# The last LayerNorm of the sample rows laid out over 128 partitions instead of 8

## The chip, the core and the metric

The kernel runs on one core of one Trainium2 chip. Its engines are TensorE (PE, matrix products), VectorE (DVE), ScalarE (ACT), GpSimd (POOL) and SyncE (SP, which here only issues DMAs). DMAs are issued by SP, ACT and POOL. The metric is the device time of one launch in microseconds (us), as the median of the runs.

## The reference, cut to what matters

One step of a one-layer decoder trunk: a mixer, a cross-attention into 256 memory tokens and a mixture of experts, with a LayerNorm behind each. It runs for a prompt of 512 tokens and for 8 sample tokens (520 rows of D = 1024 columns). The change touches only the end: the sum of each token's two experts, the residual and the last LayerNorm.

```
def layer_norm(x, g, b):
    mu = x.mean(-1, keepdims=True)
    var = jnp.mean(jnp.square(x - mu), -1, keepdims=True)
    return (x - mu) * lax.rsqrt(var + 1e-5) * g + b

x = layer_norm(ALPHA * x + hier_moe(x, p), p['ln3_g'], p['ln3_b'])
```

Each token has two chosen experts, and `hier_moe` is the weighted sum of their two outputs.

## The kernel before, in words

Tokens lie in rows. The 512 prompt rows are four tiles of 128 partitions (`t` = 0, 1, 2, 4), and the 8 sample rows are a tile of their own, number 3 (`SAMPLES`), which uses 8 of the 128 partitions. `xn[:, t, :]` holds the rows of tile `t`.

The experts run in 11 passes of 128 slots each. The outputs of the first nine passes are scattered to a table `y_d` in DRAM, one row per token and choice. The outputs of the last two passes (`KEPT`) stay in SBUF (`ysb`), and TensorE adds them to their tokens with selection matrices `places` (`add_kept` for a prompt tile, `add_samples` for the samples). A `sum_full` count tells when a bank of such sums is ready.

The rows of `y_d` reach `xn` in two ways. POOL issues accumulating DMAs (`accumulate(c, t)`, `c` is the first or second choice) in the order samples, 0, 1, 2 for the first choice, then the samples' second, tile 4's first, tile 2's second and tile 4's second; some of them wait for the landing of an earlier one of the same tile. The second choice of tiles 0 and 1 is loaded by SP into `second_choice` and added by VectorE. The semaphore `x3_in[t]` counts the landings of tile `t`.

Then comes the last norm, in the order `LAST_NORM = [0, 3, 1, 2, 4]`. For each tile VectorE adds the kept sums to `xn` in two halves of 512 columns and sums the rows in the same instruction (`tensor_tensor_reduce`, L2676). It forms minus the mean (L2681) and (x − mean)·gain (L2683). ScalarE squares with the mean as bias and sums (L1794), takes the root (L1796) and, once VectorE has the reciprocal (L2658), scales the centred rows (L1800). In the program of VectorE the reciprocal of a tile stands behind the first half of the next tile. POOL stores each scaled tile with an accumulating DMA onto output rows that already hold the bias (L3023). The last tile, 4, takes another way: VectorE scales and adds the bias in two halves (L2694), and SP and ACT store a half each (L1368, L1803).

The kept sums of the samples stand in one PSUM bank as four column groups: columns 256g to 256g + 255 of the 8 samples are on partitions 32g to 32g + 7 (L1190). Before the samples' norm, ScalarE copies two of the groups (L1790) and VectorE the other two (L2687) to 8 partitions of 1024 columns (`late_samples`).

Of the kernel before, what the change touches and what calls it, by code (L numbers as in the profile page):

```python
# [22 lines left out]
D = 1024  # L23
# [8 lines left out]
LAST_NORM = [0, 3, 1, 2, 4]  # L32
# [53 lines left out]
def rows_of(t):  # L86
    return NS if t == SAMPLES else TR
# [34 lines left out]
def layer_kernel(nc, a, o):  # L122
# [3 lines left out]
    with ctx:  # L126
# [142 lines left out]
        late_samples = P[0:NS, NT * D:(NT + 1) * D]  # L269
        zeros = view(16094, 256)  # L270
        places = smp[:, 1120:1120 + KEPT * NTOK].rearrange("p (i c) -> p i c", i=KEPT)
        tokens16 = smp[:, 2162:2162 + KEPT]
# [5 lines left out]
        kept_sums = lambda t, q: (1 if t == 0 else 2) + kept_bank(t, q)  # L278
        SAMPLES_SUM = 3
# [209 lines left out]
        def _(pe):  # L489
# [698 lines left out]
            def add_samples(i, bank):  # L1188
                for g in range(4):
                    last = mm(bank[32 * g:32 * g + NS, 0:256], places[:, i, NP_:NTOK], ysb[:, (NSCAT + i) % 3, g * 256:g * 256 + 256],  # L1190
                              start=(i == 0), stop=(i == KEPT - 1))
                return last

            pe.wait_ge(places_ready, KEPT)
# [6 lines left out]
            for t in PROMPT:  # L1201
                if t == 4:
                    pe.wait_ge(y_act, NPASS + 1)
                    pe.wait_ge(y_dve, NPASS + 1)
# [5 lines left out]
                if t == 0:  # L1210
                    add_samples(1, ps[6]).then_inc(sum_full, 1)

# [26 lines left out]
        def _(sp):  # L1239
# [129 lines left out]
            with sp.If(over > 0):  # L1369
                sp.wait_ge(x_out, 16)  # L1370
                sp.wait_ge(half_out, 16)
                sp.wait_ge(rows_out, 16 * NQT)
# [32 lines left out]
            sp.wait_ge(rows_out, 16 * NQT)  # L1405
# [11 lines left out]
        def _(act):  # L1417
# [367 lines left out]
            for i, t in enumerate(LAST_NORM):  # L1785
                n = rows_of(t)
                if t == 0:
                    act.wait_ge(sum_full, SAMPLES_SUM)
                    for g in range(2):
                        last = A(late_samples[:, g * 256:g * 256 + 256], ps[6][32 * g:32 * g + NS, 0:256], ACT.Copy)  # L1790
                    last.then_inc(y_act, 1)
                act.wait_ge(x3_mean, i + 1)
                r = rstd[0:n, t:t + 1]
                A(squares[0:n, :], xn[0:n, t, :], ACT.Square, bias=mean3[0:n, t:t + 1], accum_out=square3[0:n, t:t + 1]).then_inc(x3_square, 1)  # L1794
                act.wait_ge(x3_square, i + 2)
                A(r, square3[0:n, t:t + 1], ACT.Sqrt, scale=1.0 / D, bias=eps[0:n, :]).then_inc(x3_root, 1)  # L1796
                if i < NT - 1:
                    act.wait_ge(x3_rstd, i + 1)
                    act.wait_ge(x3_centred, i + 1)
                    A(centred3[0:n, t, :], centred3[0:n, t, :], ACT.Copy, scale=r).then_inc(x3_scaled, 1)  # L1800
# [23 lines left out]
        def _(dve):  # L1824
# [799 lines left out]
            def place_rows(i):  # L2624
                p = NSCAT + i
                dve.wait_ge(*entry_landed(p))
# [3 lines left out]
                for t in range(NT):  # L2630
                    n = rows_of(t)
# [19 lines left out]
            dve.wait_ge(gb_in, 96)  # L2651
            dve.wait_ge(xa_ready, NT)

            def take_root(i):
                t = LAST_NORM[i]
                r = rstd[0:rows_of(t), t:t + 1]
                dve.wait_ge(x3_root, i + 1)
                V.reciprocal(r, r).then_inc(x3_rstd, 1)  # L2658

            for i, t in enumerate(LAST_NORM):  # L2660
                n = rows_of(t)
                x, r = xn[0:n, t, :], rstd[0:n, t:t + 1]
                centred = centred3[0:n, t, :]
# [3 lines left out]
                for q in range(2):  # L2667
                    lo, hi = q * 512, q * 512 + 512
                    if t == SAMPLES:
                        dve.wait_ge(y_act, NPASS + 1)  # L2670
                        dve.wait_ge(y_dve, NPASS + 1)
                        total_q = late_samples[:, lo:hi]
                    else:
                        dve.wait_ge(sum_full, kept_sums(t, q))
                        total_q = ps[kept_bank(t, q)][:, :]
                    V.tensor_tensor_reduce(out=x[:, lo:hi], in0=x[:, lo:hi], in1=total_q, scale=1.0, scalar=0.0,  # L2676
                                           op0=ALU.add, op1=ALU.add, accum_out=part3[0:n, t, q:q + 1]).then_inc(row_parts, 1)
                    if q == 0 and i > 0:
                        take_root(i - 1)
                dve.wait_ge(row_parts, 2 * i + 2)  # L2680
                V.tensor_scalar(mean3[0:n, t:t + 1], part3[0:n, t, 0:1], part3[0:n, t, 1:2], -1.0 / D, ALU.add, ALU.mult).then_inc(x3_mean, 1)  # L2681
                dve.wait_ge(x3_mean, i + 1)
                V.scalar_tensor_tensor(centred, x, mean3[0:n, t:t + 1], gb[0:n, 0, :], ALU.add, ALU.mult).then_inc(x3_centred, 1)  # L2683
                if i == 0:
                    dve.wait_ge(sum_full, SAMPLES_SUM)
                    for g in (2, 3):
                        last = V.tensor_copy(late_samples[:, g * 256:g * 256 + 256], ps[6][32 * g:32 * g + NS, 0:256])  # L2687
                    last.then_inc(y_dve, 1)
                if i == NT - 1:
                    take_root(i)  # L2690
# [378 lines left out]
```

## Time and profile before

| | us |
|---|---|
| median of 3 runs | 646.45 (646.26 to 646.46) |
| the profiled execution | 650.46 |
| span of its trace | 648.6 |
| VectorE starts the first row sum of the last norm | 625.12 |
| VectorE starts with tiles 1, 2 and 4 | 631.98, 634.82, 637.66 |
| ScalarE starts the last square | 639.51 |
| ACT issues the last store | 642.81 |

All times of instructions are microseconds from the start of the span. TensorE is busy for 95% of the span, but it is done with its last sum at 635.87; the last norm, at the end, belongs to VectorE, ScalarE and the DMAs.

### The profile page before, as it was taken

The numbers are of one execution on the slowest core, as the hardware profiler recorded it, in microseconds if no ns is written. First come the engines' busy times: TensorE is split into PE (matmuls) and PEld (weight loads), VectorE is DVE, ScalarE is ACT, GpSimd is POOL, SyncE is SP. The second block draws the span as 40 slices with busy tenths as digits, with TensorE's granted clock in tenths as the row PEclk, the third lists the DMA queues.
The fourth block names the chain that finished last, engine by engine and source line by source line (L and its number), as shares of the span: only waits on it lengthen the run. The fifth ranks groups of instructions, "written<-read, shape, count | busy, mean of one in ns | idle before, by whom it ended". The sixth has DMA issues, their size and how long they took to land.

```text
span 648.6 us, 8964 instructions
## 1 busy us (share of the span) xinstructions
PE 615.8 (95%) x3319; PEld 394.6 (61%) x3319; DVE 366.7 (57%) x845; ACT 164.4 (25%) x367; POOL 204.6 (32%) x248
## 2 busy tenths in 40 slices
PE   6899999999999979999999999999999999999992
PEld 3588788887888854446888784454574443333230
DVE  1485898326556863557653874257885342443465
ACT  1175211002544120002001740221433111212144
POOL 7050010100677735312000986011324731110221
PEclk9999999999999989999999999999999999999997
DMA  8995678616335354003904985354998999999898
GB/s 278 364 312 171 235 169 229 240 51 211 118 94 214 130 195 148 16 0 107 348 1 128 340 310 200 134 225 161 369 415 326 406 411 366 334 411 418 323 185 162
DMA packets 49175, 150.08 MB, mean 231 GB/s; under 512 B 5498, under 2 KB 8250, under 8 KB 44897
## 3 DMA queue, kind: packets, MB, share of 16 engines
q1 hardware_dynamic: 35159, 112.48, 46.6%
q0 software_dynamic: 11232, 31.76, 17.4%
q10 hardware_dynamic: 2738, 5.23, 2.1%
q8 instruction: 28, 0.46, 0.3%
q14 instruction: 18, 0.15, 0.1%
HBM read 131.83 MB, written 21.90 MB: 237 GB/s over the span
## 4 chain that ended last, share of the span: by engine, by line
PE 74%; DMA 12%; DVE 7%; POOL 2%; issue 2%; SPq 2%; ACT 1%; DVEq 0%; POOLq 0%; ACTq 0%
PE ps L611 14%; PE ps L788 14%; PE ps L609 9%; PE ps L1148 7%; PE ps L517 5%; PE ps L1168 4%; DMA xn<-in_x_sample 2%; PE ps L807 2%; PE ps L890 2%; PE ps L584 2%; PE ps L874 2%; DMA xn<-y_d 1%; DMA P<-x_d,smp 1%; SPq L1273 1%; DMA wring<-in_ca_wq 1%
## 5 line engine op out<-in xcount | busy, mean ns | idle before, releaser
L788 PE MATMUL ps<-wring,P 128*128 128x512 f32 x224 | 99.2, 596 | 0.0
L788 PEld LDWEIGHTS ps<-wring,P 128*128 128x128 f32 x224 | 41.6, 190 | 49.1 <-issue 49.0
L1926 DVE SCALAR_TENSOR_TENSOR P<-ps,P 128x256 f32<-128x256 f32 (+1 forms) x83 | 33.8, 424 | 57.2 <-PE ps L611 36.6
L1148 PE MATMUL ps<-wring,P 128*32 128x512 f32 (+1 forms) x320 | 63.6, 593 | 0.9 <-DVE P L2600 0.9
L517 PE MATMUL ps<-xT,wring 128*128 128x312 f32 (+1 forms) x256 | 57.4, 383 | 0.0
L517 PEld LDWEIGHTS ps<-xT,wring 128*128 128x128 f32 x256 | 46.4, 190 | 9.3
L2600 DVE COPY P<-ps 128x512 f32<-128x512 f32 x10 | 6.9, 692 | 63.5 <-PE ps L1129 63.5
L1148 PEld LDWEIGHTS ps<-wring,P 128*32 128x32 f32 (+1 forms) x320 | 20.4, 122 | 31.0 <-issue 30.9
L2922 POOL TENSOR_TENSOR P<-P,xT 128x2048 f32<-128x2048 f32 x8 | 36.0, 4521 | 9.2 <-DMA xT<-sq_d 5.4
L2774 POOL TENSOR_SCALAR rstd<-agg 128x1 f32<-128x1 f32 (+1 forms) x10 | 12.0, 1195 | 85.3 <-DVE agg L1856 85.3
L2234 DVE SCALAR_TENSOR_TENSOR xn<-xn,ps 128x512 f32<-128x512 f32 x16 | 11.0, 684 | 42.1 <-PE ps L788 31.1
L1168 PE MATMUL ps<-P 128*32 128x512 f32 (+1 forms) x160 | 32.6, 595 | 0.7 <-issue 0.7
L609 PE MATMUL ps<-wring,P 128*128 128x256 f32 x128 | 31.1, 395 | 2.2 <-DVE wring L1901 2.2
L611 PE MATMUL ps<-xT,wring 128*128 128x264 f32 (+1 forms) x128 | 29.7, 387 | 0.1
L611 PE MATMUL ps<-P 128*128 128x264 f32 x128 | 29.5, 385 | 0.0
L611 PE MATMUL ps<-P,wring 128*128 128x256 f32 (+1 forms) x128 | 29.2, 382 | 0.0
L609 PEld LDWEIGHTS ps<-wring,P 128*128 128x128 f32 x128 | 24.7, 197 | 6.4 <-DVE wring L1901 2.6
L611 PEld LDWEIGHTS ps<-xT,wring 128*128 128x128 f32 x128 | 23.8, 190 | 5.0 <-issue 1.1
L611 PEld LDWEIGHTS ps<-P 128*128 128x128 f32 x128 | 24.3, 190 | 4.2
L1479 ACT ACTIVATE xT<-ps 128x512 f32<-128x512 f32 (+1 forms) x20 | 9.5, 515 | 67.4 <-PE ps L584 67.2
L611 PEld LDWEIGHTS ps<-P,wring 128*128 128x128 f32 x128 | 24.2, 190 | 3.8
L609 PE MATMUL ps<-P 128*128 128x256 f32 x104 | 24.3, 381 | 0.0
(480 smaller groups left out, 1157.1 us busy)
## 6 DMA issues: line engine op xcount, KB each, us to landing
wring<-in_w_in SPq DMA_DIRECT2D x5, 2048.0 KB, 9.7
wring<-in_w_gate SPq DMA_DIRECT2D x10, 1024.0 KB, 8.3
wring<-in_w_up SPq DMA_DIRECT2D x10, 1024.0 KB, 11.2
P<-in_w_down SPq DMA_DIRECT2D x10, 1024.0 KB, 11.6
P<-in_cache_mem_k SPq DMA_DIRECT2D x8, 1024.0 KB, 7.0
P<-in_cache_mem_v SPq DMA_DIRECT2D x8, 1024.0 KB, 4.9
y_d<-P POOLq DMA_DIRECT2D x1, 4160.0 KB, 32.1
wring<-in_ca_wv SPq DMA_DIRECT2D x2, 2048.0 KB, 20.0
```

The costliest lines, as they stand in the source:

```text
L517: last = mm(out, lhs(k), rhs(k), start=(k == 0), stop=(k == n - 1))
L584: last = nc.tensor.transpose(bk[:, k * n:k * n + n], xn[0:n, t, (4 * q + k) * 128:(4 * q + k + 1) * 128], ident[0:n, 0:n])
L609: last = mm(bank[:, 0:n], x[:, k, 128 * i:128 * i + 128], w[:, k, :], start=(k == 0), stop=(k == 3))
L611: last = mm(bank[:, 0:n], w[:, k, 128 * i:128 * i + 128], x[:, k, :], start=(k == 0), stop=(k == 3))
L788: last = mm(bk[:, :], src[:, k, START[t]:START[t] + TR], w[:, k, :], start=(k == 0), stop=(k == KC - 1))
L807: last = mm(bank[:, :], mixT[:, k, 0:TR], w[:, k, :], start=(k == 4), stop=(k == 1))
L874: last = mm(bk[:, 0:NM], qcT[:, 2 * h + k, t * TR:t * TR + TR], mkT[:, 2 * h + k, :], start=(k == 0), stop=(k == 1))
L890: last = mm(bk[:, 0:cn], mv[:, m, h * CE + ec * 128:h * CE + ec * 128 + 128], paT[:, h, m, c0:c0 + cn], start=(m == 0), stop=(m == 1))
L1148: last = mm(GU[p % 2][lo:lo + m, :].rearrange("p (g f) -> p g f", g=2), xgT[:, p % 3, k, lo:lo + m], gu[s][:, :, k, :], start=(k == 0), st ...
L1168: last = mm(YB[q][lo:lo + m, :], hT[:, p % 2, f, lo:lo + m], dn[s][:, f, q * 512:q * 512 + 512], start=(f == 0), stop=(f == 1))
L1926: V.scalar_tensor_tensor(dst, src, scale, part, ALU.mult, ALU.add).then_inc(part_added, 1)
L2922: G.tensor_tensor(x, x, qb[:, b % 4:b % 4 + 1].broadcast_to([128, 2, D]), ALU.mult).then_inc(kq_done, 1)
```

## The change

The samples' last norm is done in the layout in which TensorE leaves their sums: 128 partitions of 256 columns, where partitions 32g to 32g + 7 hold column group g and the other 24 partitions of each group hold zeros. The samples are third in the order: `LAST_NORM = [0, 1, 3, 2, 4]`.

- SP copies the samples' rows from `xn` to `samples_s` (128 x 256) by four SBUF-to-SBUF DMAs of 8 x 256, once the second choice has landed in them. VectorE waits for all four (`RELAID`) ahead of tile 1.
- The four copies by ScalarE and VectorE to `late_samples` are gone. VectorE adds `samples_s` and the PSUM bank in one 128 x 256 instruction ahead of tile 1.
- A row's sum is now spread over four partitions. `sum_lanes` adds the four parts on TensorE: the product of the matrix `same_lane` (1 where two partitions are equal modulo 32) with one column. This is done once for the mean, behind tile 1's sums, and once for the squares, ahead of tile 4's sums. TensorE waits for VectorE (`row_parts`) and for ScalarE (`x3_square`) before them.
- ScalarE's order is written out: the samples' square stands ahead of tile 1's scale, their root behind it, and their scale ahead of tile 2's.
- POOL sets `samples_s` to zero and loads the gain in the new layout (`gain_s`, four DMAs) during the expert passes. VectorE forms `same_lane` in the pass where it makes `places`.
- The samples are stored by four accumulating DMAs of 8 x 256 behind those of tiles 0, 1 and 2.

```
-LAST_NORM = [0, 3, 1, 2, 4]
+LAST_NORM = [0, 1, 3, 2, 4]
...
-        kept_sums = lambda t, q: (1 if t == 0 else 2) + kept_bank(t, q)
+        kept_sums = lambda t, q: {0: 1, 1: 4, 2: 7, 4: 10}[t] + q
+        SAMPLES_SUM, SAMPLES_MEAN, SAMPLES_VAR = 3, 6, 9
...
+            def sum_lanes(column, parts):
+                mm(ps[0][:, column:column + 1], same_lane, parts, start=True, stop=True).then_inc(sum_full, 1)
...
                 if t == 4:
-                    pe.wait_ge(y_act, NPASS + 1)
-                    pe.wait_ge(y_dve, NPASS + 1)
+                    pe.wait_ge(x3_square, 4)
+                    sum_lanes(1, square3[:, SAMPLES:SAMPLES + 1])
...
+                if t == 1:
+                    pe.wait_ge(row_parts, SAMPLES_ADDED)
+                    sum_lanes(0, part3[:, SAMPLES, 0:1])
...
+            sp.wait_ge(choice_in[1], 16)
+            sp.wait_ge(x3_in[SAMPLES], loads_of(SAMPLES))
+            for g in range(4):
+                sp.dma_start(samples_s[lanes(g), :], xn[0:NS, SAMPLES, quarter_of(g)]).then_inc(choice_in[1], 16)
...
+                if t == SAMPLES:
+                    dve.wait_ge(sum_full, SAMPLES_MEAN)
+                    V.tensor_scalar(mean, ps[0][:, 0:1], -1.0 / D, None, ALU.mult).then_inc(x3_mean, 1)
+                    dve.wait_ge(x3_mean, i + 1)
+                    V.scalar_tensor_tensor(centred_s, samples_s, mean, gain_s, ALU.add, ALU.mult).then_inc(x3_centred, 1)
+                    continue
+                if t == 1:
+                    dve.wait_ge(choice_in[1], RELAID)
+                    dve.wait_ge(sum_full, SAMPLES_SUM)
+                    add_rows(samples_s, ps[6][:, 0:256], part3[:, SAMPLES, 0:1])
...
+            link(G.memset(samples_s, 0.0))
+            for g in range(4):
+                pool.dma_start(gain_s[LANES * g:LANES * g + LANES, :], a["ln3_g"][0, quarter_of(g)].partition_broadcast(LANES)).then_inc(gb_in, 16)
...
+            for i, t in ((0, 0), (1, 1), (3, 2)):
                 pool.wait_ge(x3_scaled, i + 1)
+                pool.dma_start(o_xp[0, START[t]:START[t] + TR, :], centred3[:, t, :], accum_op=ALU.add).then_inc(rows_out, 16)
+            for g in range(4):
+                pool.dma_start(o_xs.rearrange("b one d -> (b one) d")[:, quarter_of(g)], centred_s[lanes(g), :], accum_op=ALU.add).then_inc(rows_out, 16)
```

On VectorE, behind the centring of tile 0 and up to the first half of tile 1, the program before has these rows (`ISA` with `ps` or `P` as its second operand is the add with row sum; the `ISA` behind it reads the sum out):

```order
L2687 COPY P<-ps 8x256 [waits sum_full]
L2687 COPY P<-ps 8x256
L2676 ISA xn,smp<-xn,P 8x512 [waits y_dve,y_act,x3_in3]
L2676 ISA smp 8x1
L2658 RECIPROCAL rstd<-rstd 128x1 [waits x3_root]
L2676 ISA xn,smp<-xn,P 8x512 [waits y_dve,y_act]
L2676 ISA smp 8x1
L2681 TENSOR_SCALAR smp<-smp 8x1 [waits row_parts]
L2683 SCALAR_TENSOR_TENSOR P<-xn,smp,gb 8x1024 [waits x3_mean]
L2676 ISA xn,smp<-xn,ps 128x512 [waits sum_full,choice_added,x3_in1]
```

On VectorE at the same place, from behind the centring of tile 0 to the first half of tile 2, the program after has these:

```order
L2701 ISA smp<-smp,ps 128x256 [waits sum_full,choice_in1]
L2701 ISA smp 128x1
L2701 ISA xn,smp<-xn,ps 128x512 [waits sum_full,choice_added,x3_in1]
L2701 ISA smp 128x1
L2698 RECIPROCAL rstd<-rstd 128x1 [waits x3_root]
L2701 ISA xn,smp<-xn,ps 128x512 [waits sum_full]
L2701 ISA smp 128x1
L2727 TENSOR_SCALAR smp<-smp 128x1 [waits row_parts]
L2729 SCALAR_TENSOR_TENSOR P<-xn,smp,gb 128x1024 [waits x3_mean]
L2708 TENSOR_SCALAR smp<-ps 128x1 [waits sum_full]
L2710 SCALAR_TENSOR_TENSOR P<-smp 128x256 [waits x3_mean]
L2701 ISA xn,smp<-xn,ps 128x512 [waits sum_full,x3_in2]
```

Nine instructions between tile 0 and tile 1 have become two, with a wait for `choice_in1`, and two small ones stand between tile 1 and tile 2. The reciprocal of tile 0 has moved behind the first half of tile 1. (In the program after, L2701 is the line of `add_rows`, and L2708 and L2710 are the samples' mean and centring.)

On SP, between the loads of the second choice (L1374) and the store of the last tile (L1384), the program after has these:

```order
L1374 DMA wring<-y_d 128x1024 [waits y_out1,y_out2,y_out0,gu_full]
L1374 DMA wring<-y_d 128x1024
L1378 DMA smp<-xn 8x256 [waits x3_in3,choice_in1]
L1378 DMA smp<-xn 8x256 x3
L1381 TENSOR_LOAD flag [waits sorted_ready]
L1381 ISA x2
L1384 DMA out<-P 128x512 [waits last_ready]
```

The two rows of L1378 are new; before, the load of the flag followed the second choice at once.

## Rows read from the trace of the kernel before

**Rows 1.** Chain that ended last: start us, us, what.
```profile
637.66 0.68 DVE xn L2676
...
640.77 0.30 ACT rstd L1796
```

**Rows 2.** Timeline, tile 1: start us, us, engine, line, operation, out<-in, count.
```profile
631.98 0.69 DVE L2676 CUSTOM_DVE_ANT_0 xn<-xn,ps 128x512 f32<-128x512 f32 x1
...
632.59 0.15 DVE L2658 RECIPROCAL rstd<-rstd 8x1 f32<-8x1 f32 x1
...
633.37 0.21 DVE L2681 TENSOR_SCALAR smp<-smp 128x1 f32<-128x1 f32 x1
...
633.83 1.13 ACT L1794 ACTIVATE P<-xn,smp 128x1024 f32<-128x1024 f32 x1
...
634.82 0.68 DVE L2676 CUSTOM_DVE_ANT_0 xn<-xn,ps 128x512 f32<-128x512 f32 x1
```

**Rows 3.** Timeline, the samples on VectorE.
```profile
628.02 0.85 DVE L2687 COPY P<-ps 8x256 f32<-8x256 f32 x2
```

**Rows 4.** Timeline, the last tile.
```profile
639.51 1.14 ACT L1794 ACTIVATE P<-xn,smp 128x1024 f32<-128x1024 f32 x1
...
642.81 0.34 ACTq L1803 DMA_DIRECT2D out<-P  x1
```

**Rows 5.** Timeline and DMA issues: out<-in queue op count, KB, us to landing.
```profile
618.66 1.69 POOL L3007 DMA_DIRECT2D xn<-y_d  x2 [2.01 <-DMA xn<-y_d]
...
xn<-y_d POOLq DMA_DIRECT2D x1, 32.0 KB, 8.8
```

**Rows 6.** Timeline and DMA issues, copies of other sizes.
```profile
612.47 0.82 SPq L1362 DMA_DIRECT2D wring<-y_d  x2
...
qk_d<-smp POOLq DMA_DIRECT2D x2, 16.0 KB, 1.8
...
wring<-y_d SPq DMA_DIRECT2D x1, 512.0 KB, 3.8
...
out<-P SPq DMA_DIRECT2D x1, 256.0 KB, 4.1
```

**Rows 7.** Traffic: PE, PEld, DVE, ACT, POOL busy (x), PEclk, DMA share, GB/s.
```profile
629.00:630.00 1.00, 1.00 (x3) 0.41 (x3) 0.96 (x4) 0.16 (x1) 0.46 (x1) 1.00 0.91 111
```

**Rows 8.** Groups by form: busy us, mean ns of one, idle before.
```profile
L2613 DVE TENSOR_TENSOR P<-P,ps 128x256 f32<-128x256 f32 x11 | 4.6, 421 | 0.4
...
L1637 ACT ACTIVATE P<-ps 128x256 f32<-128x256 f32 x16 | 6.0, 382 | 6.1 <-PE ps L890 6.1
...
L965 PE MATMUL ps<-con,smp 128*128 128x20 f32 x8 | 1.3, 238 | 0.5 <-ACT smp L1666 0.5
```

**Rows 9.** Timeline, the sums on TensorE.
```profile
625.30 10.57 PE L1186 MATMUL ps<-P,smp 128*128 128x512 f32 x24
```

**Rows 10.** TensorE waits, and clock of the stretches behind (columns of Rows 7).
```profile
31.97 3.58 PE L609 MATMUL ps<-wring,P 128*128 128x256 f32 x8 [2.18 <-DVE wring L1901]
...
32.20:35.62 3.42, 3.42 (x9) 2.71 (x9) 3.35 (x7) 1.24 (x1) 2.90 (x6) 0.50 1.07 301
...
517.15 1.06 PE L1129 MATMUL ps<-con,P 128*128 128x128 f32 x8 [1.53 <-DMA P<-x_d,smp]
...
640.00:645.00 5.00, 0.00 (x0) 0.00 (x0) 2.16 (x4) 1.03 (x3) 0.75 (x1) 0.50 1.04 208
```

**Rows 11.** Timeline and DMA issues, the stores.
```profile
634.21 0.80 POOL L3023 DMA_DIRECT2D out<-P  x1 [1.79 <-ACT P L1800]
...
639.90 0.85 POOL L3023 DMA_DIRECT2D out<-P  x1 [1.97 <-ACT P L1800]
...
out<-P POOLq DMA_DIRECT2D x1, 32.0 KB, 4.9
...
out<-P ACTq DMA_DIRECT2D x1, 256.0 KB, 3.9
```

**Rows 12.** Timeline, gather of a later pass on POOL.
```profile
542.23 1.00 POOL L2938 DMA_INDIRECT P<-x_d,smp  x1 [6.45 <-PE ps L1129]
```

More of the change, by code:

```diff
@@ L31 @@
 NQT = len(PROMPT)
-LAST_NORM = [0, 3, 1, 2, 4]
+LAST_NORM = [0, 1, 3, 2, 4]
+LANES = 32
 KC = D // 128
@@ L1404, in _ @@
             sp.wait_ge(half_out, 16)
-            sp.wait_ge(rows_out, 16 * NQT)
+            sp.wait_ge(rows_out, 16 * (NQT + 3))
             sp.wait_ge(out_done, 16 * 2)
@@ L1784, in _ @@
             act.wait_ge(x3_square, 1)
[L1785 to L1800, printed above, removed]
+            nth = LAST_NORM.index
@@ new lines, in square, with root @@
+            def square(t):
+                act.wait_ge(x3_mean, nth(t) + 1)
+                n = 128 if t == SAMPLES else rows_of(t)
+                x = samples_s if t == SAMPLES else xn[0:n, t, :]
+                A(squares[0:n, 0:x.shape[1]], x, ACT.Square, bias=mean3[0:n, t:t + 1], accum_out=square3[0:n, t:t + 1]).then_inc(x3_square, 1)
+            def root(t):
+                if t == SAMPLES:
+                    act.wait_ge(sum_full, SAMPLES_VAR)
+                    total = ps[0][:, 1:2]
+                else:
+                    act.wait_ge(x3_square, nth(t) + 2)
+                    total = square3[:, t:t + 1]
+                A(rstd[:, t:t + 1], total, ACT.Sqrt, scale=1.0 / D, bias=eps).then_inc(x3_root, 1)
@@ new lines, in scale @@
+            def scale(t):
+                act.wait_ge(x3_rstd, nth(t) + 1)
+                act.wait_ge(x3_centred, nth(t) + 1)
+                centred = centred_s if t == SAMPLES else centred3[:, t, :]
+                A(centred, centred, ACT.Copy, scale=rstd[:, t:t + 1]).then_inc(x3_scaled, 1)
+            square(0)
+            root(0)
+            scale(0)
+            square(1)
+            root(1)
+            square(SAMPLES)
+            scale(1)
+            root(SAMPLES)
+            square(2)
@@ L1801, in _ @@
+            root(2)
+            scale(SAMPLES)
+            scale(2)
+            square(4)
+            root(4)
             act.wait_ge(last_ready, 2)
@@ L2668, in _ @@
                     lo, hi = q * 512, q * 512 + 512
[L2669 to L2681, printed above, removed]
-                dve.wait_ge(x3_mean, i + 1)
[L2683 to L2688, printed above, removed]
+                    dve.wait_ge(sum_full, kept_sums(t, q))
+                    add_rows(x[:, lo:hi], ps[kept_bank(t, q)][:, :], part3[:, t, q:q + 1])
+                    if q == 0 and t != 0:
+                        take_root({1: 0, 2: 1, 4: 2}[t])
+                dve.wait_ge(row_parts, {0: 2, 1: 5, 2: 7, 4: 9}[t])
+                V.tensor_scalar(mean, part3[:, t, 0:1], part3[:, t, 1:2], -1.0 / D, ALU.add, ALU.mult).then_inc(x3_mean, 1)
+                dve.wait_ge(x3_mean, i + 1)
+                V.scalar_tensor_tensor(centred, x, mean, gb[:, 0, :], ALU.add, ALU.mult).then_inc(x3_centred, 1)
+                if t == 2:
+                    take_root(SAMPLES)
                 if i == NT - 1:
-                    take_root(i)
+                    take_root(t)
                     dve.wait_ge(x3_centred, i + 1)
@@ L3018, in _ @@
             pool.wait_ge(beta_out, 32)
-            for i, t in enumerate(LAST_NORM[:NT - 1]):
-                n = rows_of(t)
-                rows = o_xs.rearrange("b one d -> (b one) d") if t == SAMPLES else o_xp[0, START[t]:START[t] + TR, :]
+            for i, t in ((0, 0), (1, 1), (3, 2)):
                 pool.wait_ge(x3_scaled, i + 1)
-                pool.dma_start(rows, centred3[0:n, t, :], accum_op=ALU.add).then_inc(rows_out, 16)
+                pool.dma_start(o_xp[0, START[t]:START[t] + TR, :], centred3[:, t, :], accum_op=ALU.add).then_inc(rows_out, 16)
+            for g in range(4):
+                pool.dma_start(o_xs.rearrange("b one d -> (b one) d")[:, quarter_of(g)], centred_s[lanes(g), :], accum_op=ALU.add).then_inc(rows_out, 16)
             with pool.If(over > 0):
```

42 lines of the change are left out of this document (26 added, 16 removed).

## The prediction

> **What bounds the kernel now.** I read the chain that ended last first. Its end runs through the last norm: VectorE's add for tile 4, then ScalarE's square and root of that tile [rows 1]. The timeline shows why. VectorE spends 2.84 us on each prompt tile without a pause (631.98 to 634.82) [rows 2], and again on the next (634.82 to 637.66) [rows 1, 2]. It is in program order the only engine that sets the pace: TensorE works on the sums from 625.30 for 10.57 us, 24 passes of 0.44 us, eight for each of tiles 1, 2 and 4 [rows 9], so it is ahead of VectorE everywhere. The last square starts at 639.51, and ACT issues the last store 3.30 us later, at 642.81 [rows 4]; it lands 3.9 us after that [rows 11]. The last norm's length is thus the time at which that square starts.
>
> **What goes.** Between tile 0 and tile 1 VectorE has the samples' two copies and their norm, from 628.02 to 631.98 [rows 2, 3], 3.96 us. After the change it has one 128 x 256 add there, 0.42 us by the nearest form [rows 8], and between tiles 1 and 2 a 128 x 1 mean (0.21 us [rows 2]) and a 128 x 256 centring (0.42 [rows 8]), 0.65 in all. Alone this is 3.96 − 0.42 − 0.65 = 2.9 us less for VectorE. ScalarE's two copies stand ahead of tile 0's square, for whose mean it waits anyway; their going is worth nothing.
>
> **What is added, and when it can start.** Ahead of tile 1 VectorE now waits for four copies that SP may issue only when the samples' second choice has landed. POOL issues that accumulation at 618.66, and it lands 8.8 us later, at 627.5 [rows 5]. Before, this was hidden: the samples' add stood behind VectorE's copies, which end at 628.87 [rows 3]. Now a second DMA hangs on the first. SP takes a landing up within 0.1 us and issues two DMAs in 0.82 us, 0.41 each [rows 6], so the four start at 627.55, 627.96, 628.37 and 628.78. Call the landing of the last one R. No copy of 8 KB inside SBUF by SP is in the trace. From below, a 16 KB DMA of POOL's queue took 1.8 us [rows 6]: R = 630.6. From above, SP's last 256 KB store took 4.1 us with busy DMA engines [rows 6]: R = 632.9. Between them stands SP's 512 KB load in a quiet stretch, 3.8 us [rows 6]; it carries 64 times the bytes, so I put a quiet copy of SP at 2.5, nearer to the small DMA than to this one. From 629 on tile 2's second accumulation fills 0.91 of the DMA engines [rows 7], for which I add 0.2. I take 2.7 us, R = 631.5. VectorE, ready at 628.0, stands 3.5 us, and all that was saved is spent.
>
> The trace has a small DMA at 1.8 us and a larger one at 3.8. The Trainium skill (DMA: Bandwidth & Descriptors, "Anatomy of one DMA — SWDGE (gpsimd) path") gives about 2.0 us fixed for each DMA on POOL's path and the rest by bytes. By it R would be 630.8 and the whole 0.7 us shorter than what I forecast; it is an estimate, and these four are on SP's path.
>
> **From R to the last square.** In a tile's block the reciprocal comes 0.61 us after the start, the mean 1.39, ScalarE's square 1.85 and the next block 2.84 [rows 2]. Square and root take 1.26 + 0.30 = 1.56 us [rows 1, 4].
> - VectorE: samples' add at R, tile 1 from R + 0.5, samples' mean at R + 3.3, tile 2 from R + 4.0, tile 4 from R + 6.9.
> - TensorE: tile 1's sums are done at 625.30 + 8 x 0.44 = 628.8. Then it waits for the samples' add. A product with few columns takes 0.24 us [rows 8], with the weight load some 0.35: tile 2's sums run from R + 0.9 to R + 4.3, in time for VectorE.
> - ScalarE: tile 1's square at R + 2.3, root done at R + 3.9, then the samples' square (0.38 by a 128 x 256 form [rows 8], and its read-out), done at R + 4.4. Only then may TensorE form the second product, and only behind that tile 4's sums: R + 4.8 to R + 8.3, readable some 0.1 later. ScalarE goes on with tile 1's scale, samples' root and tile 2's square and root, done at R + 7.7.
> - VectorE could do the second half of tile 4 at R + 7.8, but has its sum at R + 8.45. From there to the last square it is 1.85 − 0.69 = 1.16 us [rows 2]: R + 9.6.
>
> With R = 631.5 the last square starts at 641.1 instead of 639.51: +1.6 us. Of this, 0.6 comes from TensorE, which was never late before and now waits twice.
>
> **What lies elsewhere.** POOL's zeroing and four gain loads, some 3 us of POOL time, stand in front of gathers of later passes; one of those waited 6.45 us for TensorE [rows 12], so I count nothing. If that cover were gone it would be at most those 3 us. VectorE's two extra instructions for the lane matrix fall into a pass that TensorE bounds: nothing. Wider sample products (32 columns for 8) have the same pass length. The samples' stores: POOL took 0.80 us for a 32 KB one, and issued tile 2's at 639.90 [rows 11]. Now tile 2's comes at about 641.2 and the last of four more at 641.2 + 0.85 + 3 x 0.80 = 644.5; it lands between 1.8 and 4.9 us later [rows 6, 11], 646.3 to 649.4. The last store of ACT lands at 641.1 + 3.3 + 3.9 = 648.3. I count nothing, and up to 1.1 us at the upper end.
>
> **Sum.** The profiled execution took 650.46 us with a span of 648.6; the last store would end 1.6 later: 652.0 for it. The median of the runs, 646.45, lies 4.0 below the profiled execution; I carry the difference over: 648.0. With the bounds of R (−0.9, +1.4) the forecast's own range is 647.1 to 649.5. A measurement of this kernel can tell 0.2%, 1.3 us, from no change.
>
> **The rivals.**
> - *TensorE's clock falls.* TensorE would idle from 628.8 to R + 0.5 = 632.0, 3.2 us, in the middle of its work, where it had no pause. In the trace a pause of 2.18 us was followed by a stretch at 0.50 of full clock, a pause of 1.53 us was not, and from 640 on, some 4 us after TensorE's last product, the clock is at 0.50 too [rows 10]. For it: 3.2 is beyond 2.18. Against: two pauses are few, and where the fall would come relative to the work is open. At 0.50 the eight passes of tile 2 (3.45 us) run at 0.87 each until the clock is back; over 3.4 us at that level, as long as the stretch shown [rows 10], 1.7 us of work are lost, and some 1.0 if the fall comes before the work resumes. VectorE has 0.3 us to spare, and tile 4's sums come late by the rest and a little: +1.0 to +1.7 on the last square, 649.4 in all. The Trainium skill (TensorE: Matmul & The Clock Gate, "What's actually happening") has the slow level as the default that activity lifts; by that rule, too, the new pause invites the fall.
> - *The copies are hidden: faster.* If they were in SBUF by 628.0, tile 1 would start at 628.5 and the last square at 628.0 + 9.6 = 637.6 or slightly later, −1.9 us: 644.6. It needs the samples' second accumulation to land 3 us earlier, or R below 629.9, where the gain starts. The last copy alone is issued at 628.78, so even 1.8 us is too much. Against it speaks every row; for it only that the landing at 627.5 is one reading of one execution.
> - *A wash.* R near 630.6, by the short end: 631.5 − 630.6 = 0.9 less, +0.7, 647.1. With a slack of some tenths in ScalarE's chain it is 646.8.
> - *The samples' stores end last.* As above, 1.1 us on top of 648.0: 649.1.
>
> **Chances.** Forecast 0.45, clock 0.28, wash 0.14, stores 0.05, hidden 0.08. Slower by over 0.2% (above 647.74) are the clock case, the stores and two thirds of the forecast's: 0.28 + 0.05 + 0.29 = 0.62. Within 0.2%: 0.14 + 0.16 = 0.30. Faster: 0.08. The range leaves out the hidden case and the top of the clock case: 646.6 to 650.0.
>
> **What would show it.** In the changed profile: four SPq issues right behind 627.5; an idle time of VectorE of 2.5 to 4.5 us ahead of the 128 x 256 add, put down to a DMA into `smp`; TensorE idle from 628.8 until about 632; a wait of VectorE ahead of the second half of tile 4; the last square near 641. It is wrong if the copies land within 1 us of issue, if the samples' accumulation lands well before 627, or if the granted clock between 632 and 640 shows 0.50, which is the first rival.

## The result, and the profile after

The changed kernel takes 657.46 us (median of 6 runs, 653.57 to 659.61) against 647.26 for the kernel before on the same chip (6 runs, 646.26 to 653.14): ratio 1.013, 95% interval 1.010 to 1.0161. It is slower, as forecast, but by some 8 us by the ratio where 1.6 were forecast, and outside the range of 646.6 to 650.0. (The two medians lie 10.2 us apart, which is the upper end of that interval; the runs of the kernel before spread over 6.9 us.) The profiled execution took 657.39 us (span 655.7) against 650.46 (648.6): 6.9 us more.

| us from the start of the span | before | changed |
|---|---|---|
| POOL issues the first accumulation into `xn` | 612.99 | 612.54 |
| VectorE's first row sum of the last norm | 625.12 | 624.48 |
| ScalarE starts the last square | 639.51 | 644.59 |
| ACT issues its last store | 642.81 | 647.90 |
| from the last square to the end of the span | 9.09 | 11.11 |

The span grew by 7.1 us: 5.1 ahead of the last square, 2.0 behind it. The chain that ended last now runs through SP's four copies (start us, us, what):

```profile
618.03 8.22 DMA xn<-y_d
...
626.32 0.82 SPq L1378
...
629.06 3.47 DMA smp<-xn
...
633.04 0.58 PE ps L1201 x2
633.62 6.31 PE ps L1192 x8
...
644.43 0.85 POOL out L3067
645.29 0.91 POOL out L3069 x2
...
646.56 2.00 POOL out L3069
```

The samples' second accumulation lands at 626.25, and SP starts at once. Its fourth issue begins only at 629.06, 2.74 us after the first (forecast 1.23), and 3.47 us more pass to the landing (forecast 2.7). The four copies as a relay, from 626.32 to 632.53, thus take 6.2 us instead of 3.9. The timeline has both waits on it, VectorE's and TensorE's, in the last column:

```profile
626.32 3.37 SPq L1378 DMA_DIRECT2D smp<-xn  x4
...
632.55 0.42 DVE L2701 CUSTOM_DVE_ANT_0 smp<-smp,ps 128x256 f32<-128x256 f32 x1 [5.21 <-DMA smp<-xn]
...
633.04 0.58 PE L1201 MATMUL ps<-smp 128*128 128x1 f32 x2 [4.50 <-DVE smp L2701]
...
633.48 6.43 PE L1192 MATMUL ps<-P,smp 128*128 128x512 f32 x8
...
637.39 0.69 DVE L2701 CUSTOM_DVE_ANT_0 xn<-xn,ps 128x512 f32<-128x512 f32 x1 [0.97 <-PE ps L1192]
...
639.95 0.69 DVE L2701 CUSTOM_DVE_ANT_0 xn<-xn,ps 128x512 f32<-128x512 f32 x1 [1.79 <-PE ps L1192]
...
643.61 0.69 DVE L2701 CUSTOM_DVE_ANT_0 xn<-xn,ps 128x512 f32<-128x512 f32 x1 [0.65 <-PE ps L1192]
```

TensorE, which worked without a pause before [rows 9], stands for 4.50 us. Tile 2's eight passes then take 6.43 us; eight took 3.5 before [rows 9]. VectorE waits for them twice, 2.8 us in all, and once more ahead of tile 4's second half, 0.65. The stretches show why (columns of Rows 7; PEclk, the third number from the end, is the granted clock as a share of full speed):

```profile
629.00:631.00 2.00, 0.00 (x0) 0.00 (x0) 0.00 (x0) 0.00 (x0) 0.75 (x1) 1.00 1.09 203
631.00:633.00 2.00, 0.00 (x0) 0.00 (x0) 0.45 (x3) 0.00 (x0) 0.00 (x0) 0.80 1.03 184
633.00:636.50 3.50, 3.46 (x6) 1.92 (x7) 3.31 (x9) 2.77 (x5) 0.87 (x1) 0.50 0.18 34
636.50:640.00 3.50, 3.50 (x8) 1.47 (x8) 0.82 (x4) 1.45 (x3) 0.36 (x1) 0.64 0.90 150
640.00:643.00 3.00, 3.00 (x9) 1.30 (x8) 2.89 (x8) 2.20 (x6) 0.49 (x1) 1.00 0.75 111
```

The clock falls in the pause and is at 0.50, its lower level of 1.2 GHz, when the work resumes: the first rival of the prediction. At the end POOL issues five stores where it had one left (they answer to [rows 11]; the second fence is from the DMA issues, with KB and us to landing):

```profile
644.43 0.85 POOL L3067 DMA_DIRECT2D out<-P  x1 [3.94 <-ACT P L1822]
...
644.97 3.59 POOL L3069 DMA_DIRECT2D out<-P  x4
...
647.90 0.34 ACTq L1840 DMA_DIRECT2D out<-P  x1
```

```profile
out<-P POOLq DMA_DIRECT2D x4, 8.0 KB, 4.7
```

The chain ends with POOL's issues, at 648.56. The last of the four is issued from about 647.7 and takes 5.5 us to land (4.7 is the median of the four), so it is down at about 653, and the span ends some 2 us behind that, as it did behind ACT's half before (landed at 646.7, span 648.6). ACT's half, issued at 647.90, has landed by 651.9. The samples' stores end last.

### The profile page after: what moved, and what is told of

Its sections match the earlier page's. It is cut to its first block, busy times and chain, and to the rows that moved or that the text cites. A ratio compares the mean times of both kernels' runs of the same rounds, so it can differ in the third digit from the quotient of the medians.

```text
span 655.7 us, 8979 instructions
## 1 busy us (share of the span) xinstructions
PE 621.3 (95%) x3323; PEld 396.4 (60%) x3323; DVE 365.0 (56%) x843; ACT 162.4 (25%) x365; POOL 208.9 (32%) x256
## 4 chain that ended last, share of the span: by engine, by line
PE 78%; DMA 8%; DVE 6%; POOL 2%; SPq 2%; ACT 2%; issue 1%; POOLq 0%; DVEq 0%; ACTq 0%
PE ps L617 15%; PE ps L794 14%; PE ps L1154 11%; PE ps L615 7%; PE ps L523 5%; PE ps L1174 5%; DMA xn<-in_x_sample 2%; PE ps L813 2%; DMA xn<-y_d 2%; PE ps L896 2%; PE ps L1026 2%; PE ps L590 2%; PE ps L880 1%; PE ps L1135 1%; PE ps L803 1%; DMA y_d<-P,smp 1%
## 5 line engine op out<-in xcount | busy, mean ns | idle before, releaser
L1154 PE MATMUL ps<-wring,P 128*32 128x512 f32 (+1 forms) x320 | 66.4, 603 | 0.9 <-DVE P L2637 0.9
L2817 POOL TENSOR_SCALAR rstd<-agg 128x1 f32<-128x1 f32 (+1 forms) x10 | 11.9, 1194 | 86.8 <-DVE agg L1893 86.8
L2271 DVE SCALAR_TENSOR_TENSOR xn<-xn,ps 128x512 f32<-128x512 f32 x16 | 10.9, 684 | 43.8 <-PE ps L794 33.0
L615 PE MATMUL ps<-wring,P 128*128 128x256 f32 x128 | 29.5, 380 | 1.2 <-DVE wring L1938 1.2
## 6 DMA issues: line engine op xcount, KB each, us to landing
y_d<-P POOLq DMA_DIRECT2D x1, 4160.0 KB, 31.8
```

The source lines that it names most:

```text
L615: last = mm(bank[:, 0:n], x[:, k, 128 * i:128 * i + 128], w[:, k, :], start=(k == 0), stop=(k == 3))
L1154: last = mm(GU[p % 2][lo:lo + m, :].rearrange("p (g f) -> p g f", g=2), xgT[:, p % 3, k, lo:lo + m], gu[s][:, :, k, :], start=(k == 0), st ...
```

## The experiments

Theory A, from this profile: three costs, that the copies are late, that the clock falls in the pause this makes, and that the four stores end last. Rival B: the new order of the tiles costs the time. Rival C: the product with one column and the wider sums on TensorE do. All runs stand against the kernel before on their own chip. Since executions differ by up to 6 us in when the last norm begins, for reasons that lie ahead of it, the traces are compared by stretches: F is VectorE's first row sum of the last norm, S the last square. The ratios come from all runs of a kernel, the stretches from its one profiled execution.

| kernel | ratio (95%) | F to S | S to end | F to end |
|---|---|---|---|---|
| before | 1 | 14.4 | 9.1 | 23.5 |
| changed | 1.013 (1.010, 1.016) | 20.1 | 11.1 | 31.2 |
| c1_after | 1.0122 (1.0091, 1.0153) | 19.8 | 10.8 | 30.6 |
| c0_before | 1.0001 (0.9974, 1.0028) | 14.5 | 8.9 | 23.4 |
| e4_order | 0.9983 (0.9953, 1.0012) | 15.0 | 9.1 | 24.1 |
| e2_input | 1.0028 (1.0007, 1.005) | 13.1 | 10.9 | 23.9 |
| e5_input_one | 0.9996 (0.9973, 1.0018) | 13.6 | 9.8 | 23.3 |
| e3_one_store | 1.0098 (1.0068, 1.0128) | 19.4 | 9.7 | 29.1 |
| e1_fill | 1.011 (1.0081, 1.0139) | 17.0 | 10.8 | 27.8 |
| e6_dram_late | 1.0087 (1.0058, 1.0117) | 20.5 | 11.0 | 31.5 |
| e7_quiet | 1.0075 (1.0034, 1.0116) | 16.4 | 11.8 | 28.2 |
| v1_direct | 1.0036 (1.0011, 1.0061) | 12.0 | 8.9 | 20.9 |
| v2_early | 1.0103 (1.0083, 1.0124) | 14.3 | 8.8 | 23.1 |
| v3_split | 1.0027 (1.0000, 1.0055) | 14.0 | 10.5 | 24.5 |

c1_after is the changed kernel once more. c0_before is the kernel before with an empty line more in its source.

> The changed kernel once more, for the comparison on this chip. My account of its first profile splits what it loses against the kernel before into three terms: VectorE stands for the four copies of the samples' rows (some 5 us, where 2.9 us of work were saved), TensorE's clock falls in the pause (2.5 us on the last square), and the samples' four stores end after the last tile's (1.4 us). Expected here: 1.0 to 1.6% slower than before, with the last square 11.5 to 12.5 us behind the last copy's landing. If the terms were noise of one profile, the pause and the clock at 0.50 would not come again.

> The kernel before once more, for a second trace. From VectorE's first add of the last norm to the last square it took 14.4 us and to the end of the span 23.5 us; expected within 0.5 us of both, with the start of that stretch moved by up to 4 us, as the starts of the other runs are. If the stretch itself varied by more than 1 us, the terms that I read from single profiles would not be worth their numbers.

Both came out as the kernels they repeat, and the pause and the clock at 0.50 came again. But c1_after's last square lay 11.1 us behind the last copy's landing and not 11.5 to 12.5 as expected, where the changed kernel's lay 12.06: that stretch alone varies by 1 us.

**The order alone** (the kernel before):

```
-LAST_NORM = [0, 3, 1, 2, 4]
+LAST_NORM = [0, 1, 3, 2, 4]
```

> The kernel before with the order of tiles changed alone: LAST_NORM = [0, 1, 3, 2, 4], the samples in their old layout of 8 partitions. Theory (the order costs nothing by itself, all loss is in the new layout's waits): the last square within 0.5 us of 26.5 us after POOL's first accumulation and no change of the time beyond 0.3%. Rival (the order is part of the loss, since tile 1 and then tile 2 are asked for earlier than their rows land): 1 us or more slower.

No difference beyond the uncertainty. Rival B falls. The trace missed its mark: the last square came 29.8 us after POOL's first accumulation and not within 0.5 of 26.5. Most of that lies ahead of the new order, since F came 14.9 us after the accumulation instead of 12.1; the 15.0 us from F on hold 0.64 us of VectorE's waits for TensorE, and less these they are the 14.4 of before within 0.1.

**No late copies.** The four copies take the kernel's input rows, early, and wait for nothing late:

```
-            sp.wait_ge(x3_in[SAMPLES], loads_of(SAMPLES))
+            sp.wait_ge(gb_in, 160)
...
-                sp.dma_start(samples_s[lanes(g), :], xn[0:NS, SAMPLES, quarter_of(g)])...
+                sp.dma_start(samples_s[lanes(g), :], a["x_sample"]...[:, quarter_of(g)])...
```

> SP fills the samples' layout from the rows of the input x_sample, as soon as tile 1's second choice is loaded, instead of copying the summed rows after the second accumulation; the samples' output leaves out the residual and the scattered choices. Same four DMAs of 8x256, off the path. Theory (the wait for the copies is the largest term): VectorE goes from tile 0 to the samples' add without a pause, TensorE has no pause over 1 us and its clock stays, the time falls by 6 to 8 us against the changed kernel and stands within 2 us of the kernel before; tile 4 can't start before its second accumulation lands (some 5.5 us after its issue at about 629), so VectorE gains at most 1.4 us on the kernel before. Rival (the new waits between TensorE and VectorE or the stores carry the loss): the time falls by less than 3 us.

0.94% less than the changed kernel (1.0028 against 1.0122 of c1_after), some 6 us, as the theory had it, and the two intervals do not meet. TensorE has no pause (the column for the releaser is empty) and its passes are back at full speed:

```profile
629.03 0.28 PE L1201 MATMUL ps<-smp 128*128 128x1 f32 x2
629.17 3.68 PE L1192 MATMUL ps<-P,smp 128*128 128x512 f32 x8
```

The one-column products are all still in this kernel, so rival C falls too: two of them take 0.28 us, and F to S is 1.3 us shorter than before. The end is not short: S to end is 1.8 us longer than before.

**One store of the samples instead of four** (`for g in range(1)` at L3068), once with the late copies, once with the early ones of e2_input:

> Only the first of the samples' four stores is issued; columns 256 to 1023 of the samples' output keep the bias alone. Theory (the stores' tail is 1.4 us): the run ends with the landing of ACT's half of tile 4, and the time falls by 1.0 to 2.0 us. Rival (the stores are hidden behind tile 4's own): no change beyond 0.5 us.

> Both edits together: the samples' layout is filled early from the input's rows, and only the first of the samples' four stores is issued (the samples' output leaves out residual, scattered choices and three quarters of the columns). The early rows alone brought the last square to 25.0 us after POOL's first accumulation (26.5 in the kernel before) but the span then still ran 10.9 us from the last square (9.1 before). Theory (the stores of POOL are the whole difference at the end): 9.1 to 9.7 us from the last square, 34.2 to 34.8 us from POOL's first accumulation to the end of the span, 0.8 to 1.4 us less than the kernel before. Rival (the end is long for another reason, such as the DMA traffic that is packed closer): 10.5 us or more again.

By the ratios three stores cost 0.24% with the late copies and 0.32% with the early ones, 1.6 and 2.1 us, about what was expected; each pair of intervals overlaps, but the traces say the same, S to end is 1.1 us shorter in both. With early copies and one store the time is that of the kernel before (0.9996; the 0.8 to 1.4 us below it that I expected don't show): late copies, what follows from them, and stores together are the whole loss. S to end is still 0.7 us longer than before in both (9.8 and 9.7 against 9.1); one of the four stores is left there, and what the 0.7 us are was not tried.

**The pause filled.** Four more products of tile 2's selection, into a bank that is read by nobody, stand ahead of TensorE's wait for the samples:

```
+                    for _ in range(4):
+                        add_kept(0, ps[7], t, 0, start=True, stop=True)
                     pe.wait_ge(row_parts, SAMPLES_ADDED)
```

> Four more 128x512 products (3.4 us of TensorE's time) into a bank that is overwritten later stand ahead of TensorE's wait for the samples' add. Nothing else changes. Theory (the clock's fall costs 2.5 us): the granted clock stays at 1.00 until the last sum, tile 2's and tile 4's sums take 3.5 us each, the last square comes 9.6 us behind the last copy's landing instead of 12.06, and the time falls by 2 to 3 us against the changed kernel. Rival (the clock only shadows the waits of VectorE, the chain runs over ScalarE): the clock stays up and the time stays within 0.5 us.

TensorE worked on into 637.30, 1.3 us beyond the samples' add at 635.96, so the fill itself held it up a little:

```profile
630.33 7.13 PE L1192 MATMUL ps<-P,smp 128*128 128x512 f32 x16
...
637.30 0.28 PE L1201 MATMUL ps<-smp 128*128 128x1 f32 x2
637.44 3.68 PE L1192 MATMUL ps<-P,smp 128*128 128x512 f32 x8
```

The clock was 1.00 in every stretch from 628 to 646. From the landing of the copies to the last square it took 9.85 us; with the pause it was 12.06 (changed), 12.08 (e6_dram_late, below), 11.1 (c1_after) and 10.7 (e3_one_store). The fall of the clock costs 0.9 to 2.2 us of that stretch by these, and 1.4 to 2.8 against the 9.3 us of e7_quiet, below, which has no filler in the way. In the time of the runs this doesn't stand out of the uncertainty (1.011 against 1.0122): the 2 to 3 us that I expected are not shown. Nor is the 17.0 of F to S in the table the gain of the filler, since in this execution F itself came 13.5 us after POOL's first accumulation instead of 11.9 (changed). Counted from that accumulation, the last square came at 30.6 us instead of 32.0 (changed) and 31.8 (c1_after).

**What makes the relay slow.** In e6_dram_late the four copies start as late as in the changed kernel, but read the input rows in DRAM instead of `xn`. In e7_quiet they read `xn`, and the second accumulations of tiles 2 and 4, which POOL issues in the same microseconds, are left out.

> The changed kernel with one edit: the four copies still wait for the samples' second accumulation, but read the rows of the input x_sample in DRAM instead of xn in SBUF (the samples' output leaves out residual and scattered choices). In the changed kernel SP took 3.3 to 3.5 us to issue the four and the last landed 6.2 to 7.1 us after the first issue; from DRAM and 9 us earlier in the program it took 1.5 us. Theory (a source in SBUF makes these issues slow): 1.5 to 1.8 us for the four and a landing some 4.5 us after the first issue, the time 1.5 to 2 us under the changed kernel. Rival (POOL's own DMA issues or the full queues at that moment slow them): 3 us or more for the four and a landing after 6 us or more, as in the changed kernel.

> The changed kernel without POOL's last two accumulations, the second choice of tiles 2 and 4 (their output leaves it out); one of them is issued in the same microsecond as SP's four copies, the other before the last of the copies lands. In the changed kernel the last copy lands 6.2 to 7.1 us after the first issue; with a source in DRAM the four issues took 1.4 instead of 3.3 us, but the landing came only some 0.6 us sooner. Theory (the copies' small packets wait behind the 512 KB accumulations in the DMA engines): the last copy lands within 4.5 us of the first issue, VectorE starts the samples' add 2 us or more earlier, and the time falls by 2 to 4 us against the changed kernel, part of it since tiles 2 and 4 need no second landing. Rival (a fixed cost of each copy inside SBUF): 6 us or more again.

The chains of c1_after, e6_dram_late and e7_quiet, SP's issues and then the copy's way:

```profile
626.65 0.82 SPq L1378
627.53 0.64 SPq L1378
628.21 0.88 SPq L1378
...
629.13 3.87 DMA smp<-xn
```

```profile
626.62 0.35 SPq L1378
627.01 0.35 SPq L1378
627.41 0.29 SPq L1378
627.75 4.50 DMA smp<-in_x_sample
```

```profile
626.74 0.82 SPq L1378
...
627.62 0.64 SPq L1378
...
628.30 0.62 SPq L1378
...
628.96 1.78 DMA smp<-xn
```

From the first issue to the landing it is 6.35, 5.6 and 4.0 us. The quiet relay is the one that I had forecast, 3.9 us, though its parts are not: each issue is slower, the way is shorter. Two things are apart here. An issue takes SP 0.6 to 0.8 us in e7_quiet, where both ends are in SBUF, and 0.3 to 0.35 in e6_dram_late, where the source is in DRAM. There the issues came out by the theory, but the landing, 5.6 us after the first issue, lies nearer to the rival. (By the ratios, 1.0087 against 1.0122, that is 2.3 us less, but the intervals overlap.) The way from the last issue on takes 1.8 us when the DMA engines are idle and 3.5 to 4.5 when they are full. The issues are not quite free of the traffic either: the third of the four took 0.62 us in e7_quiet, but 0.88 to 1.32 in the changed kernel, c1_after and e3_one_store. Why the third, no run shows.

The slow issue does not go with a source in SBUF as such. v1_direct, below, stores the samples by SP from SBUF to DRAM in pieces of the same 8 KB, 0.30 to 0.39 us each, with the DMA engines full. What the slow ones share is that both ends are in SBUF:

```profile
639.82 1.45 SPq L1392 DMA_DIRECT2D out<-P  x4
```

In e7_quiet TensorE's pause is 2.94 us, and no stretch up to 643 shows a lower clock (the third row, from the stretches, has the idle DMA engines, 0.05):

```profile
631.25 0.38 PE L1201 MATMUL ps<-smp 128*128 128x1 f32 x2 [2.94 <-DVE smp L2701]
631.49 3.68 PE L1192 MATMUL ps<-P,smp 128*128 128x512 f32 x8
...
628.00:631.00 3.00, 0.31 (x1) 0.00 (x0) 0.24 (x1) 0.00 (x0) 0.00 (x0) 1.00 0.05 11
```

From the landing to the last square it took 9.3 us. F to S is 3.4 us shorter than in c1_after: 2.35 by the relay and 1.84 by the stretch behind it, less 0.8 since the samples' second accumulation landed later after F. By the ratios it is 0.47%, 3 us, within the 2 to 4 expected, but the two intervals overlap.

**Three whole kernels without the late relay.** v1_direct copies the samples' residual into the lanes early (these copies don't wait for any choice), loads their two choices from `y_d` and the bias straight into the lanes, lets VectorE add them, and stores the samples by SP without accumulation, as soon as they are scaled:

```
+            for c in range(2):
+                for g in range(4):
+                    sp.dma_start(choices_s[lanes(g), c, :], y_choice[c, NP_:NTOK, quarter_of(g)]).then_inc(choice_in[1], 16)
+            for g in range(4):
+                sp.dma_start(bias_s[LANES * g:LANES * g + LANES, :], ...).then_inc(choice_in[1], 16)
...
+                if t == 1:
+                    dve.wait_ge(choice_in[1], 64 + 16 + 128 + 64)
+                    for c in range(2):
+                        link(V.tensor_tensor(samples_s, samples_s, choices_s[:, c, :], ALU.add))
```

v2_early loads the bias early and puts the eight loads of choices ahead of the two tile loads into `second_choice`. v3_split loads the bias early, leaves the order of the loads, and moves VectorE's wait for the samples to where they are first used.

> The full computation with the new layout and without its late copy. SP copies the samples' residual into the layout before the last pass ends and loads both scattered choices straight from y_d into it (eight DMAs of 8x256, behind tile 1's second choice); VectorE adds them in the pause in which it waits for tile 1's first choice; POOL no longer accumulates for the samples. VectorE scales the samples and adds the bias itself, and SP stores them. Theory: no pause of VectorE or TensorE over 1 us, the last square 24.5 to 25.5 us after POOL's first accumulation, 9.1 to 9.7 us from there to the end, so 1 to 2 us less than the kernel before (0.15 to 0.3%). Rival (the twelve small DMAs delay the tiles' rows, or VectorE's extra adds fall on the path): no gain or a loss.

> The version with the samples loaded straight into the new layout, with two groups of DMAs moved: the bias in the new layout is loaded before the last pass ends, and the eight DMAs of the samples' choices are issued ahead of the tiles' second choice instead of behind it. In the first form VectorE stood 4.1 us for the bias before its first add of the last norm, which ate all that the shorter norm gained (20.9 us from that add to the end of the span, against 23.5 in the kernel before). Theory: the first add comes 12 to 13 us after POOL's first accumulation again, tile 2 then waits for its second accumulation, and the time is 0.8 to 2 us under the kernel before (0.1 to 0.3%). Rival (the eight DMAs push the tiles' rows back by as much): no gain.

> As v1_direct (the whole computation; the samples' residual, their two choices and the bias are loaded straight into the 128 lanes by SyncE, and SyncE stores the samples), with two things moved: the bias is loaded before the choices instead of as the last of thirteen small copies, and VectorE waits for the samples' copies where it first adds them, not ahead of tile 1's rows. In v1_direct VectorE stood 4.06 us before tile 1's add, and its first add of the last norm began 16.13 us after GpSimd's first accumulation, against 11.9 to 12.1 in the kernels without that wait. Theory A (the small copies are slow while the tiles' rows are moving, and what is waited for behind them is late): the first add comes 12 us after the first accumulation, from there to the end 21 to 23 us (v1_direct 20.9), the tail 33 to 35 us against 35.6 of the kernel before, the median 1 to 2.5 us below it (ratio 0.996 to 0.999), TensorE at its full clock in the last norm. Rival B (the eight copies of the choices themselves land at about 627.6, whatever stands behind them): VectorE's wait of 3 to 4 us only moves behind tile 0, TensorE pauses over 4 us, its clock falls to 0.50 as in the changed kernel and in v2_early, and the time is that of v1_direct or worse (ratio 1.003 to 1.010).

v1_direct has the shortest last norm of all, 20.9 us from F to the end, and loses that ahead of F:

```profile
617.15 2.31 SPq L1385 DMA_DIRECT2D P<-in_ln_b  x4
...
627.60 0.89 DVE L2700 TENSOR_TENSOR smp<-smp,P 128x256 f32<-128x256 f32 x2 [4.06 <-DMA P<-in_ln_b]
```

The bias, which doesn't depend on anything, is the last of twelve small DMAs behind the tiles' rows (the expectation for v3_split counts thirteen) and lands 8.6 us after its issue. TensorE pauses for 3.06 us here, with the clock at 1.00 all the same. v2_early shows the same for the rows that stand behind the small ones:

```profile
616.61 12.11 DMA wring<-y_d
628.75 0.44 DVE smp L2700
...
634.07 0.58 PE ps L1202 x2
634.65 5.81 PE ps L1193 x8
```

Tile 1's rows are issued some 3 us later than before and arrive 12.1 us after that (tile 0's took 8.6). They stand behind the eight small loads, but by then POOL has issued the first of its 512 KB accumulations too, and no run tells the one from the other. TensorE pauses again, for 4.56 us, its clock is at 0.50 from 634 to 637, and the kernel is 1.0% slower. v3_split removes the wait: VectorE adds the choices at 626.62 without standing, and F comes 11.6 us after POOL's first accumulation, where it was 16.1 in v1_direct and 12.1 before. But it now stands for tile 2's rows, and the chain says so:

```profile
613.41 13.21 DMA xn<-y_d
...
626.91 5.56 DMA xn<-y_d
...
632.50 0.69 DVE xn L2711
```

F to S is 14.0, hardly better than the 14.4 before, and the time is not shown to differ from before in either direction to speak of (1.0000 to 1.0055). Of theory A the first add and the clock came true; the 21 to 23 us from F to the end (24.5) and the gain did not. v1_direct and v2_early ended as their rivals had it, without a gain. I read from the stretches that little is left to win here. In e2_input, whose last square came 1.5 us sooner after the first accumulation than before (25.0 against 26.5), the DMA engines were full to the end (the second number from the end is their busy share):

```profile
634.00:637.00 3.00, 2.51 (x6) 0.76 (x4) 2.35 (x6) 2.97 (x6) 0.86 (x1) 1.00 1.06 202
637.00:640.00 3.00, 0.00 (x0) 0.00 (x0) 2.51 (x6) 1.61 (x4) 2.63 (x5) 1.00 1.06 172
640.00:643.00 3.00, 0.00 (x0) 0.00 (x0) 0.81 (x2) 0.00 (x0) 1.51 (x2) 0.77 1.02 236
```

The kernel before has a slack of a quarter in such a stretch:

```profile
637.00:640.00 3.00, 0.00 (x0) 0.00 (x0) 2.93 (x8) 2.73 (x5) 0.98 (x2) 0.96 0.76 96
```

A shorter norm may push its stores into engines that are full. That is a reading, and two runs speak against its simplest form. e7_quiet has neither of the last two accumulations, and its engines are full at that point all the same, with stores alone; its S to end, 11.8 us, is the longest of all:

```profile
640.00:643.00 3.00, 0.00 (x0) 0.00 (x0) 2.57 (x4) 1.54 (x3) 3.00 (x5) 1.00 1.04 167
```

And v1_direct has the engines 0.87 to 0.98 busy from 640 to 646 and yet 8.9 us. What lengthens the end beyond POOL's stores of the samples stays open. No version beat the kernel before.

## Why the prediction was wrong

The direction and most of the mechanism were right: the wait of VectorE for SP's copies, put down to `smp<-xn`; TensorE late for the first time; a wait ahead of tile 4's second half (0.65 us). What goes was right as well: with the copies out of the way (e2_input) F to S is 1.3 us shorter; I had put 1.9 for that case. POOL's gain loads and zeroing and the wider products cost nothing that shows, since e5_input_one has them all and takes the time of the kernel before. The failed steps, against the 6.9 us between the two profiled executions, of which I had 1.6:

- *"The four start at 627.55, 627.96, 628.37 and 628.78", "I take 2.7 us".* The relay took 6.2 us and not 3.9, +2.3. In part (+1.5) the row was the wrong neighbour: 0.41 us an issue was read from loads out of DRAM, and copies inside SBUF took 0.6 to 0.8, the third 1.15. In part (+0.8) the way was the wrong size: the quiet copy that I put at 2.5 us takes 1.8, and the traffic for which "I add 0.2" made 3.5 to 3.9 out of it. The samples' second accumulation landed 1.25 us earlier than the row of before said (626.25 for 627.5), so that R moved by only 1.0, from 631.5 to 632.5; it lay inside the bounds (632.9). That was luck: the early landing hid half of what the relay cost more.
- *"R + 9.6".* It held where the clock did: 9.3 in e7_quiet, 9.85 in e1_fill. In the changed kernel it was 12.06, +2.5, and 11.1 in its repetition, +1.5. This is the first rival, which I had at 0.28 and +1.0 to +1.7. The Trainium skill (TensorE: Matmul & The Clock Gate, "What's actually happening") has the slow level as the default that activity lifts, and the traces agree: 0.50 after pauses of 4.50 to 5.51 us, 1.00 when the pause was filled. The longer relay made the pause longer than the 3.2 us that I argued from. Pauses of 2.94 us (e7_quiet) and 3.06 (v1_direct), near that, left the clock at 1.00: the two misses go together. Had the relay taken my 3.9 us, the forecast case could have stood; but since 2.18 us were followed by 0.50 in the kernel before [rows 10], the length of the pause alone doesn't decide it.
- *"I count nothing, and up to 1.1 us at the upper end"* for the stores. S to end grew by 2.0 us. An issue took 0.90 us and not 0.80 (3.59 for four), and the first began at 644.97, behind tile 2's store, which the late norm had pushed back as well. By e3_one_store and e5_input_one 1.1 us of it are three of the stores in the traces, and 1.6 to 2.1 in the ratios, where the intervals overlap; the rest of the 2.0 is not shown. It was a price that I had worked out and then not charged.

Together 1.0 + 2.5 + 2.0 = 5.5 us beyond the 1.6, for 5.3 that were missing. The profiled execution of before, 650.46 us, was 3.2 us longer than the median of its kernel on that chip, which is why the ratio of the runs shows more, 8 us. The range failed because I kept the rivals apart, each alone on top of the forecast: a late landing lengthens the pause that lets the clock fall, and both push the stores back, so these prices add up. The stores' own price comes even without the other two: in e2_input nothing is late and the clock stays, and S to end is 1.8 us longer than before.

The rival "hidden" (−1.9) could not have reached its 644.6 even with the copies in time: e2_input has them in time and is not faster. I had not asked what was late next, and that is the samples' stores.

## What to carry to other kernels

A small DMA put between the landing of another and the engine that waits for the data costs its issues plus its way, and both are to be priced from a row with the same two ends (SBUF or DRAM) and the same traffic; four of them in a row behind the last data were worth more than the 3 us of vector work that they saved. A pause of TensorE in the middle of its work is to be priced with its clock, and the trace of a run with a filler in the pause shows how much that is, even where the time of the runs doesn't. Where risks share a cause, add them up for the upper end of the range.

## What the runs showed of the hardware that I had not expected

- SyncE took 0.6 to 1.3 us to issue an 8 KB copy inside SBUF (3.37 for four; 2.85 for four at 605 us in v1_direct, in another place of the program, with the DMA engines full) and 0.3 to 0.35 to issue one from DRAM into the same buffer (1.43 for four). An 8 KB store from SBUF to DRAM took it 0.30 to 0.39 (v1_direct).
- An 8 KB copy inside SBUF landed 1.78 us after its issue began with the DMA engines 0.05 busy, and after 3.47 to 3.98 us with engines 1.0 to 1.1 busy (changed, c1_after, e3_one_store); out of DRAM it was 4.50 (e6_dram_late).
- Two 512 KB loads that were issued 3 us later than before, behind eight loads of 8 KB and POOL's first accumulations, landed 8.6 and 12.1 us after issue (v2_early); ahead of them the median was 3.4 to 4.4.
- POOL took 0.90 us to issue an accumulating store of 8 KB (3.59 for four) and 0.85 for one of 512 KB.
- TensorE's clock stayed at 1.00 over pauses of 2.94 us (e7_quiet) and 3.06 (v1_direct), and was at 0.50 after pauses of 4.50, 4.56, 4.78, 4.89 and 5.51 us, but also after one of 2.18 in the kernel before [rows 10]. The eight passes behind those long pauses took 5.1 to 6.5 us instead of 3.7.
